# Cross attention of a decoder trunk: probabilities turned in two pairs, and the first output chunk placed between the second pair and the last two heads' values

## What is computed

```python
XATTN_HEADS = 4
XATTN_HEAD_DIM = D_MODEL // XATTN_HEADS

def cross_attention(h, memn, wq, wkv, wo):
    bsz, seq, _ = h.shape
    m = memn.shape[1]
    q = (h @ wq).reshape(bsz, seq, XATTN_HEADS, XATTN_HEAD_DIM)
    kv = (memn @ wkv).reshape(bsz, m, 2, XATTN_HEADS, XATTN_HEAD_DIM)
    s = jnp.einsum('bshd,bmhd->bhsm', q, kv[:, :, 0]).astype(jnp.float32) * (XATTN_HEAD_DIM ** -0.5)
    p = jax.nn.softmax(s, axis=-1).astype(h.dtype)
    o = jnp.einsum('bhsm,bmhd->bshd', p, kv[:, :, 1]).reshape(bsz, seq, XATTN_HEADS * XATTN_HEAD_DIM)
    return o @ wo
```

## Time and profile before

| | us |
|---|---|
| three runs | 1206.83, 1207.28, 1207.35 |
| median | 1207.28 |
| span of the profiled execution, first to last instruction | 1206.8 |
| TensorE busy | 1198.2 |
| VectorE busy | 793.3 |
| ScalarE busy | 644.4 |
| GpSimd busy | 118.7 |

### The profile page before, as it was taken

The page is one execution under the profiler, slowest core; times in us unless marked ns, Lnnn a source line. Parts: engine busy times, 40 slices in busy tenths (PEclk is TensorE's granted clock), DMA queues, the critical chain, the costliest instruction groups (busy, mean ns, idle before and its releaser), DMA issues.

```text
span 1206.8 us, 17690 instructions
## 1 busy us (share of the span) xinstructions
PE 1198.2 (99%) x7013; PEld 1046.9 (87%) x7013; DVE 793.3 (66%) x841; ACT 644.4 (53%) x873; POOL 118.7 (10%) x104
## 2 busy tenths in 40 slices
PE   9999999999999999999999999999999999999997
PEld 8888889889989888888888888899878898888886
DVE  6766766865657676666676665667785676656664
ACT  6554546553556554454564444454666565544443
POOL 1000001640142020000020000020001121100001
PEclk9999999999999999999999999999999999999999
DMA  9966755554444466565556565654642435755560
GB/s 316 323 219 177 203 180 173 161 158 143 140 160 148 140 210 198 183 196 187 174 177 207 184 198 177 204 168 152 205 133 76 129 118 162 240 180 202 177 205 35
DMA packets 164880, 214.74 MB, mean 178 GB/s; under 512 B 14816, under 2 KB 140896, under 8 KB 164704
## 3 DMA queue, kind: packets, MB, share of 16 engines
q1 hardware_dynamic: 164544, 213.29, 54.7%
q0 software_dynamic: 144, 0.52, 0.1%
q10 hardware_dynamic: 144, 0.26, 0.1%
HBM read 213.02 MB, written 1.05 MB: 177 GB/s over the span
## 4 chain that ended last, share of the span: by engine, by line
PE 98%; DVE 0%; DMA 0%; POOL 0%; ACT 0%; issue 0%; POOLq 0%; DVEq 0%
PE ps L1991 30%; PE ps L1998 16%; PE ps L1970 15%; PE ps L1971 15%; PE ps L1972 15%; PE ps L2055 1%; PE ps L2644 1%; PE ps L2666 1%; PE ps L2511 0%; PE ps L2608 0%; PE ps L2605 0%; DMA arena<-in_first 0%; PE ps L2266 0%; PE ps L2118 0%; PE ps L2367 0%; PE ps L2389 0%
## 5 line engine op out<-in xcount | busy, mean ns | idle before, releaser
L1991 PE MATMUL ps<-hT,w_hi 128*128 128x512 f32 x1568 | 376.3, 392 | 1.0 <-ACT w_hi L746 0.8
L1991 PEld LDWEIGHTS ps<-hT,w_hi 128*128 128x128 f32 x1568 | 291.0, 189 | 59.4 <-DVE hT L1274 1.1
L1389 DVE TENSOR_TENSOR w_lo<-raw,w_hi 128x2048 fp32r<-128x2048 f32 x108 | 247.6, 2292 | 62.0 <-ACT w_hi L827 62.0
L1234 DVE TENSOR_TENSOR w_lo<-raw,w_hi 128x2048 fp32r<-128x2048 f32 x85 | 195.2, 2307 | 72.3 <-ACT w_hi L697 72.2
L1998 PEld LDWEIGHTS ps<-hT,w_lo 128*128 128x128 f32 x1568 | 202.1, 192 | 8.2
L697 ACT ACTIVATE w_hi<-raw 128x2048 fp32r<-128x2048 f32 x85 | 162.2, 1914 | 86.6 <-PE ps L1972 86.0
L827 ACT ACTIVATE w_hi<-raw 128x2048 fp32r<-128x2048 f32 x108 | 206.0, 1907 | 0.6 <-DMA raw<-in_ffn_w_gate 0.6
L1998 PE MATMUL ps<-hT,w_lo 128*128 128x256 f32 x1568 | 204.4, 283 | 0.0
L1970 PE MATMUL ps<-w_hi,arena_r 128*128 128x512 f32 x354 | 138.3, 391 | 0.0
L1971 PE MATMUL ps<-w_lo,arena_r 128*128 128x512 f32 x354 | 137.8, 389 | 0.0
L1972 PE MATMUL ps<-w_hi,arena_r 128*128 128x512 f32 x354 | 137.4, 388 | 0.0
(11 more groups left out here) (316 smaller groups left out, 1634.0 us busy)
## 6 DMA issues: line engine op xcount, KB each, us to landing
raw<-in_ffn_w_down SPq DMA_DIRECT2D x44, 1024.0 KB, 4.9
raw<-in_ffn_w_gate SPq DMA_DIRECT2D x43, 1024.0 KB, 5.3
raw<-in_ffn_w_up SPq DMA_DIRECT2D x43, 1024.0 KB, 5.3
raw<-in_xattn_wkv SPq DMA_DIRECT2D x16, 1024.0 KB, 5.4
raw<-in_even_w_in SPq DMA_DIRECT2D x13, 1024.0 KB, 5.2
raw<-in_xattn_wq SPq DMA_DIRECT2D x8, 1024.0 KB, 5.1
raw<-in_xattn_wo SPq DMA_DIRECT2D x8, 1024.0 KB, 4.9
raw<-in_odd_w_in SPq DMA_DIRECT2D x6, 1024.0 KB, 5.5
```

Source lines behind the costliest of these rows:

```text
L1234: ins = V.tensor_tensor(lo, src, hi.bitcast(F32), ALU.subtract)
L1389: V.tensor_tensor(w_lo[:, m % RING, :], raw[:, m % RING, :], w_hi[:, m % RING, :].bitcast(F32), ALU.subtract).then_inc(lo_done, 1)
L1991: mm(ps[:, bank0 + m, :], cols(w_hi, n, k, CW, m * P, (m + 1) * P), hT[:, k, :, :].rearrange("p a c -> p (a c)"), start=k == 0, stop=False)
```

## The change

The order of the steps of `cross(layer)` is changed on three engines. TensorE turns heads 0 and 1 one behind the other, before the last scores, then heads 2 and 3 one behind the other, behind the values of heads 0 and 1; the first output chunk comes next, and the values of heads 2 and 3 stand between the first and the second output chunk. ScalarE copies the outputs of heads 0 and 1 before the turned probabilities of heads 2 and 3. VectorE takes the low parts of heads 0 and 1 together, before the probabilities of head 2 and the maxima of head 3, and makes the low part of the second output chunk's weights (`lo_upto(wo + 2)`) before the outputs of heads 2 and 3.

```diff
@@ -947,11 +947,12 @@
                 exponentials(2)
                 probs_out(u, 1)
                 exponentials(3)
+                heads_out(0)
+                heads_out(1)
                 probs_out(u, 2)
-                heads_out(0)
                 probs_out(u, 3)
-                for h in range(1, XH):
-                    heads_out(h)
+                heads_out(2)
+                heads_out(3)
                 hi_upto(wq + 7)
@@ -1496,14 +1497,18 @@
                 queries_lo(3)
                 maxima(2)
                 turned_lo(0)
+                turned_lo(1)
+                probabilities(2)
                 maxima(3)
-                probabilities(2)
-                turned_lo(1)
                 probabilities(3)
+                b = OT_BASE[f"cross{layer}"]
+                oT_lo(b + 1, 0, 0)
+                oT_lo(b + 2, 2, 1)
                 turned_lo(2)
                 turned_lo(3)
-                for h in range(XH):
-                    oT_lo(OT_BASE[f"cross{layer}"] + h + 1, 2 * h, h)
+                lo_upto(wo + 2)
+                oT_lo(b + 3, 4, 2)
+                oT_lo(b + 4, 6, 3)
                 add_residual(wo + 3, 1.0, ("norm", layer, 3))
@@ -2286,18 +2291,22 @@
                 project(3)
                 scores(2)
                 turned(0)
+                turned(1)
                 scores(3)
-                turned(1)
                 values(0)
+                values(1)
                 turned(2)
-                values(1)
                 turned(3)
-                values(2)
-                values(3)
                 b = OT_BASE[f"cross{layer}"]
                 key = ("norm", layer, 3)
-                out_chunks(wo, lambda i: pe.wait_ge(oT_done, b + i + 1),
-                           between=turn_ahead(norm_no(layer, 3), key), order=turn_order(key))
+
+                def head_ready(i):
+                    if i == 1:
+                        values(2)
+                        values(3)
+                    pe.wait_ge(oT_done, b + i + 1)
+
+                out_chunks(wo, head_ready, between=turn_ahead(norm_no(layer, 3), key), order=turn_order(key))
```

## The result

| | before | after |
|---|---|---|
| median of 11 runs, us | 1207.41 | 1210.17 |
| lowest to highest | 1206.83 to 1208.52 | 1209.76 to 1212.02 |
| ratio, 95% interval | | 1.0023 (1.0015 to 1.0030) |
| span of the profiled execution | 1206.8 | 1208.4 |

A forecast was written before the change was run, and what follows sets the result against it. TensorE's own stream was taken as the bound. Per layer, 0.53 us of waits gone, 0.03 to 0.06 for pairing and joins, 1.72 and 0.26 of new waits; over two layers +2.9 us, 1210.2 us, range 1208.9 to 1211.4.

The forecast's parts named there:

- third chunk's low part ready: VectorE finishes the third chunk's weights at 406.0; TensorE wants them at 406.5, a cover of 0.5 us.
- later per layer: Third output chunk starts at 406.55 instead of 405.06 in layer 0, 1.49 us later; layer 1 the same.
- What is there to gain: TensorE, from head 0's turning to the first output chunk: 0.53 us of waiting, all this order can give back.
- The three places that I named: TensorE waits: head 2's transposes 0.18 instead of 0.12, head 1's values 0.60 not 0.35, head 3's values 0.26 not 0.12.
- Pairing costs nothing: Two groups of four transposes joined into eight on TensorE cost 0.03 us a pair; could be worth +-0.1 us.
- The new wait, 1.72 us: TensorE turns head 3 at 392.08, not 390.36, waiting for VectorE's product; list entry near 3.5 us in all.
- A second entry of 0.5 us for the first chunk: TensorE's first output chunk waits 0.26 us a layer for head 0's low part; a new group in the waits list.
- Second wait, for the third chunk's weights: Rival: the 0.5 us cover is gone, TensorE waits 0.2 to 0.8 us a layer more, 1210.6 to 1211.8; chance 0.12.
- Not slower: Rival: head 3's product done by 390.36, no new wait, gain of 0.5 us a layer, 1206.3; chance 0.04.
- The clock: Rival: the new wait makes TensorE's granted clock fall from 2.4 to 1.2 GHz; chance 0.03.
- The clock's price: With the clock fallen, 24 matmuls of the chunk behind the wait take twice as long: +5.4 us a layer, 1221.
- Span and median: Whole run: profiled span 1206.8 becomes 1209.7; the median lies 0.5 above the span, so 1210.2 was forecast.

The follow-up runs named there:

- spread: Changed kernel with one output chunk between values of heads 1 and 2, another between those of heads 2 and 3, helpers reordered to match; 1206.12 us.
- one_by_one: max3_early with the first pair undone: TensorE turns head 0, makes head 3's scores, then turns head 1; 1206.46 us.
- max3_early: Changed kernel with VectorE's maxima of head 3 moved before the low part of head 1 and the probabilities of head 2; 1206.71 us.
- late_weights: Changed kernel with the low part of the second output chunk's weights made behind the outputs of heads 2 and 3 on VectorE; 1221.66 us.
- wait_2us: Changed kernel with the reduction of head 3's maxima made twice on VectorE, same output; 1213.61 us.
- wait_3us: Changed kernel with the reduction of head 3's maxima made three times on VectorE, same output; 1216.14 us.

## Why the prediction was right

By its own steps, with 1.43 added to the times after:

| step | forecast | measured |
|---|---|---|
| values of head 0 | 387.01 | 386.97 |
| low part of head 1 | 387.53 | 387.50 |
| head 3's reduction | 388.94 | 388.91 |
| head 3's product | 391.34 | 391.26 |
| head 3 turned | 392.08 | 392.01 |
| first chunk | 392.69 | 392.61 |
| values of head 2 | 398.22 | 398.20 |
| third chunk | 406.55 | 406.54 |
| third chunk's low part ready | 406.0 | 406.00 |
| later per layer | 1.49 | 1.48 |

- *What is there to gain.* 0.53 us of waits a layer was the whole of it; spread took 0.52. The three places that I named add up to 0.45 only. The rest lies in the matmuls right behind them: the second one of head 3's values, for one, comes at 392.83, 0.22 behind the first instead of 0.12.
- *Pairing costs nothing.* Held for the first pair (one_by_one: 0.16 us the other way, through head 1's low part). From the first of eight transposes to the second matmul behind them it is 0.99, where I had 1.03 from a row of twelve.
- *The new wait, 1.72 us.* From start to start of the two groups of transposes it is 2.16. Four transposes take 0.44 of it (the next matmul comes 0.79 behind the first of eight and 0.35 behind the first of four), which leaves 1.72. The profile's list says 1.56, since it counts from the modelled end of the last transpose. I had asked for a list entry near 3.5 us; it shows 3.1. A second entry of 0.5 us for the first chunk did not appear: that delay, 391.18 instead of 390.93 (0.35 behind the transposes), is hidden beneath the modelled end of the transposes.
- *Cause.* Shown by max3_early: one step moved on VectorE takes back all of it, 1.60 us a layer against a loss of 1.48.
- *Second wait, for the third chunk's weights.* Did not come; the cover was 0.54 us (ready 404.57, asked 405.11). The load behind this low part went out at 404.60, 406.03 with the 1.43, and ScalarE came to its weights at 412.24, held up by TensorE: hidden, as forecast. That the weights can bound this stretch is shown by late_weights, for the second chunk.
- *Not slower.* Refuted by the 2.8 us.
- *The clock.* It did not fall, but the step that gave it 0.03 was wrong, and that it did no harm was luck: I compared 1.72 us with a stretch of 2.00 us without matmuls near the end of the run that had the full clock. A length of idleness that once left the clock alone is no bound: 2.29 us let it fall in one layer of two. I also looked only at the idle stretch itself, and the fall can show later. TensorE's last matmul of that profile starts at 1200.23, and the clock falls at 1205.1, in the next stretch of the same list:

```profile
1204.00:1207.00 3.00, 0.00 (x0) 0.00 (x0) 0.00 (x0) 0.00 (x0) 0.00 (x0) 0.68 0.65 240
```

- *The clock's price.* It was wrong too: I had all 24 matmuls of the chunk at half speed, 5.4 us a layer and 1221 in all. The runs show 1.2 GHz for 3.4 us, which costs 1.5 to 1.7 us a layer; a wait of 1.7 us with such a fall in both layers would have given 1213 to 1214 (an estimate: 1210.2 and twice 1.5 to 1.7). The change came through with 0.7 us to spare at most: one reduction more on VectorE, in wait_2us, made it 1213.6.
- *Span and median.* I set the median 0.5 above the span of the profile before. By the runs that list both, a time lies 1.8 to 2.5 above its own span; the profiled execution of before was a late starter, which hid 1.5 of that. It did no harm, as the sum was a difference laid on the median.

What is left open: why some executions start late (the slow pace of the first matmuls is seen, its cause not tried), and what decides whether the clock falls: it didn't behind 1.56 us, and behind 2.29 us it did in one layer and not in the other.

## What to carry to other kernels

When TensorE's order is changed, write down for each step of the helpers when its input is ready and what stands ahead of it in its queue; here VectorE waited for one head's copy with another head's ready softmax behind it, and so turned its own slack into TensorE's idle time. A long independent piece (here an output chunk of 5.45 us) hid a hand-over only where it stood between the release of the chain and its use; behind the wait it hid nothing. TensorE is hardly ever idle here, and rows of start times predicted each step of this move to 0.1 us. What is left to gain is the sum of the gaps, to be counted before anything is moved.

## What the runs showed of the hardware

- The granted clock fell behind waits of TensorE of 3.70 us and 3.02 us (both layers each) and of 2.29 us (one of two), and stayed at 1.2 GHz for some 3.4 us each time: 1.5 to 1.7 us on top of the wait. It can fall when TensorE is at work again: 1.4 us after its restart in layer 0 of late_weights (restart 403.18, fall 404.6), 1.2 and 1.6 us after it in wait_3us, 0.5 us after it in wait_2us. In layer 1 of late_weights it fell 0.5 us before the restart. So the clock is to be read in the stretches behind a wait too, and not in the wait alone.
- Executions of one kernel come in two groups, about 1.5 us apart, by how fast the first matmuls go (12 or 21 in the same 4 us; two of the eleven profiles have 12). What makes them slow was not tried. A profile can fall in either, so that two profiled spans (here 1206.8 and 1208.4) can understate or overstate a difference of 2.9.
